# The PSUM banks of attention given out anew, with sample updates and window 0 re-spaced, in a two-layer hybrid decoder step

## The chip, the cores and the metric

One core of a Trainium2 chip runs the whole step in one launch. The metric is the time of one execution on the device in microseconds (us), median of several runs. The kernel is written engine by engine: TensorE (PE; its weight loads are shown apart as PEld), VectorE (DVE), ScalarE (ACT), and SyncE (SP), whose queue starts most transfers. Each engine works off its own instructions strictly in order, and all waiting between engines is by semaphores set by hand. GpSimd has nothing to do in the stretches below.

## The reference, cut to what matters

One inference step over 1024 new prompt tokens and 32 sample tokens (8 sequences of 4), width 1024, all in fp32. Layer 0 is gated linear attention (4 heads) and a convolutional feed-forward layer; layer 1 is sliding-window attention (window 128, 16 heads of 64, 2 key/value heads, a learned bias, one sink per head) and another conv-FFN. Every sub-layer has a norm before and after it. The parts touched:

```python
def step(S, inp):                       # linear attention, per chunk
    ...
    S_new = jnp.exp(b_last)[..., None] * S + jnp.einsum('bchk,bchv->bhkv', k_dec, vi)
...
def sink_attend(q, k, v, bias, valid, sinks):
    s = jnp.einsum('bqngd,bknd->bngqk', q, k).astype(jnp.float32) * ATT_HEAD_DIM ** -0.5 + bias
    s = jnp.where(valid, s, -jnp.inf)
    m = jnp.maximum(jnp.max(s, axis=-1, keepdims=True), sink)
    p = jnp.exp(s - m)
    denom = jnp.sum(p, axis=-1, keepdims=True) + jnp.exp(sink - m)
    return jnp.einsum('bngqk,bknd->bqngd', (p / denom).astype(v.dtype), v)
```

The output of attention goes through an output projection (w_o_b) and is added to the residual stream after a norm.

## The kernel before, in words

**Matrix products.** Every fp32 product is made of three matmuls in the reduced type fp32r: low weights by high activations, high by low, high by high. The weights come as 366 blocks of 128 x 1024. For each, SP loads it (w_load, L407, a ring of two), ACT rounds it to the high half (w_round, L415), DVE subtracts to get the low half (w_rest, L420); high and low have a ring of three blocks. `project` (L431, matmuls L437) multiplies one block by the token stream; `down_unit` (L450, L460) makes one unit of an output (down) projection from two blocks into one PSUM bank, and `down_add` (L464, L470 and L472) has DVE add it to the accumulator. Tokens stand in two halves, X = 0 (512 tokens, one chunk) and X = 1 (512 and the 32 samples, two chunks of 272). PSUM has 8 banks, PS[:, 0] to PS[:, 7].

**Linear attention.** Eight turns u: 4 heads times 2 halves; in turns 4 to 7 (X = 1) each of the 8 sample sequences also updates its state. On PE, `turn` (L698) ends with outputs, then `sample_deltas` (L781, L788) for sequences 0 to 3, half of the next turn's first value projection, sequences 4 to 7, the sum of squares over partitions (L844 to L847, matmuls with ones, L846; it waits for DVE's fold, gq_f) and the second half of the projection. The products alternate between banks 6 and 7, so product b waits for update b-2. DVE makes the eight updates (L1049 to L1053, L1052), then the fold (L1055). ACT goes on with the norm's logarithm and exponential (L1242, L1244). In the last turn the first FFN block stands in the place of the next projection (`pe_first_block`).

**Attention.** 64 steps, g: 16 pairs of heads q (8 for each half of the tokens, since X = 0 and X = 1 are walked one after the other) times 4 blocks of 128 tokens. The loop over steps s (L1751) makes windows of 8 steps, s = 8k + w. On PE step s has scores(s) (L1630, banks 0 and 1), a part of a query projection if w < 4 (query 2k+1 in w = 0, 1; 2k+2 in w = 2, 3; L437, banks 5 and 6), transposed(s-2) of the probabilities (L1642, banks 2 and 3 in turn), a quarter of the output projection of window k-1 if w >= 4 (downs, L1660, banks 6 and 7 in turn, each waiting until the unit two before has been added), and values(s-3) (L1656, bank 4). DVE has lo(s-4) (L1832, low half of the output), divided(s-1) (L1825, the reciprocal), biased(s) (L1818: adds the bias and takes the negated maximum in one reduction; L1811 copies the sink), low halves of weights, and the accumulations. ACT has hi(s-4) (L1998), scaled(s-1) (L1976, probabilities by the reciprocal), exps(s) (L1967, which waits until transposed(s-2) has read the same buffer, tf), turned(s-2) (L1989, transposed probabilities from PSUM to SBUF), query copies (L1955), and the roundings of weights. In the windows from k = 4 the norm of a half is interleaved with this by tables (ACT_AT, DVE_AT, PE_AT, L1580 to L1590): squares and roots, with the table loads of Ln and Exp on ACT (L520, L522).

**Sample softmax.** In windows k = 4 to 7 (d = k - 4) the 32 sample tokens' attention over their caches stands among the steps, all as one tile of 128 x 1056. PE: s_scores (L1710) in w = 4, 5, s_transposed (L1732, L1734) in w = 0 to 2 of the next window, s_values (L1743). DVE: s_new (L1847), s_add (L1853), s_masked (L1859, L1861) in w = 5, 6, s_max (L1865 to L1870) in w = 7, s_scaled (L1874 to L1878) in w = 0 of the next window, after the two low halves of output weights. ACT: s_exps (L2020, L2021) in w = 7, after the roundings of `downs_done`.

**The head of attention.** act_att (L1939) begins with the rounding of a query block, the roundings behind layer 0's last down projections (`act_ffn_downs_done`), the wait for the convolution state's output, and only then query(0). SP (sp_rest, L2128), at the block ("aq", 0, 2), waits for the last down projection of layer 0 (dn_full) before it loads the attention bias (L2088) and constants (L2152), whose buffers lie on the FFN's; the weight blocks behind stand in the same queue.

## Time and profile before

| | us |
|---|---|
| median of 3 runs (lowest, highest) | 2677.86 (2673.72, 2679.54) |
| the profiled execution, its own time | 2676.1 |
| its span in the trace | 2674.3 |
| PE busy | 2510.8 (94% of the span) |
| PEld busy | 2195.8 (82%) |
| DVE busy | 1624.0 (61%) |
| ACT busy | 1145.8 (43%) |
| mean granted clock of TensorE | 0.971 |

The linear attention takes about the first 700 us, the first conv-FFN runs to 1429, attention from there to about 1890, the second conv-FFN to the end. A row "PE banks L1732 <- DVE s_scores L1878: 6.8, 2, 3.8" in the view of waits says that PE, before instructions of line 1732 that write banks, waited 6.8 us in all in 2 places, the longest 3.8, for DVE's line 1878. In a timeline each row has start, duration, engine, line, operation, out<-in and count, and in brackets the idle time before it and who ended it.

### The profile page before, as it was taken

How to read it: one execution, taken by the hardware profiler on the slowest of the kernel's cores; microseconds unless marked ns; L12 is line 12 of the kernel's file. 1: busy time of each engine (PE TensorE's matmuls, PEld its weight loads, DVE VectorE, ACT ScalarE, POOL GpSimd, SP SyncE). 2: the span in 40 equal slices, each digit the busy share in tenths (PEclk: the TensorE clock that was granted, in tenths of full speed). 3: DMA queues.
4: the chain of work that ended last, by engine and by line, in shares of the span. 5: the costliest groups of instructions: out<-in, count | busy, mean ns of one | idle time of the engine just before them, and what ended most of it. 6: DMA issues, size and time to landing. Idle time of an engine off the chain costs nothing. (4 is left out here: it accounts for less than half of the span.)

```text
span 2674.3 us, 37812 instructions
## 1 busy us (share of the span) xinstructions
PE 2510.8 (94%) x15455; PEld 2195.8 (82%) x15455; DVE 1624.0 (61%) x2928; ACT 1145.8 (43%) x1810; POOL 0.2 (0%) x4
## 2 busy tenths in 40 slices
PE   7999999998999999999997899888999999999997
PEld 5778888887778889999996577766788888999996
DVE  5676656575656556766655655564676555655556
ACT  5554453443443334343334656563434333323333
POOL 0000000000000000000000000000000000000000
PEclk9999999899999999999998899999999999999999
DMA  4221222223433323322323222230342322333222
GB/s 153 65 77 64 88 95 84 95 81 109 149 102 109 100 91 101 133 80 95 95 76 102 90 92 64 85 97 26 107 146 93 95 95 95 103 119 95 87 87 95
DMA packets 93434, 255.18 MB, mean 95 GB/s; under 512 B 12500, under 2 KB 43709, under 8 KB 91325
## 3 DMA queue, kind: packets, MB, share of 16 engines
q1 hardware_dynamic: 69980, 209.24, 24.6%
q10 hardware_dynamic: 23280, 43.52, 4.7%
q8 instruction: 123, 2.02, 0.3%
q14 instruction: 51, 0.41, 0.1%
HBM read 225.92 MB, written 26.74 MB: 94 GB/s over the span
## 5 line engine op out<-in xcount | busy, mean ns | idle before, releaser
L437 PE MATMUL banks<-act_hi,w_lo 128*128 128x272 f32 (+1 forms) x2952 | 984.1, 333 | 29.8 <-DVE w_lo L420 13.0
L437 PE MATMUL banks<-act_hi,w_hi 128*128 128x272 f32 (+1 forms) x2952 | 969.1, 328 | 0.0
L437 PE MATMUL banks<-act_lo,w_hi 128*128 128x272 f32 (+1 forms) x2952 | 967.7, 328 | 0.0
L415 ACT ACTIVATE w_hi<-w_raw 128x1024 fp32r<-128x1024 f32 x366 | 380.7, 1055 | 716.5 <-PE banks L460 491.1
L420 DVE TENSOR_TENSOR w_lo<-w_raw,w_hi 128x1024 fp32r<-128x1024 f32 x366 | 442.7, 1223 | 395.9 <-ACT w_hi L415 395.5
L437 PEld LDWEIGHTS banks<-act_hi,w_lo 128*128 128x128 f32 x2952 | 567.0, 192 | 96.2 <-issue 33.5
L437 PEld LDWEIGHTS banks<-act_lo,w_hi 128*128 128x128 f32 x2952 | 567.9, 192 | 44.6 <-issue 1.7
L437 PEld LDWEIGHTS banks<-act_hi,w_hi 128*128 128x128 f32 x2952 | 566.3, 192 | 44.9
L472 DVE TENSOR_TENSOR acc<-acc,banks 128x272 f32<-128x272 f32 (+1 forms) x624 | 315.3, 519 | 194.4 <-PE banks L460 191.2
L460 PE MATMUL banks<-h_hi,w_lo 128*128 128x272 f32 (+1 forms) x1056 | 346.2, 328 | 25.5 <-DVE acc L472 12.6
L460 PE MATMUL banks<-h_hi,w_hi 128*128 128x272 f32 (+1 forms) x1056 | 344.2, 326 | 0.0
L460 PE MATMUL banks<-h_lo,w_hi 128*128 128x272 f32 (+1 forms) x1056 | 343.8, 326 | 0.0
L460 PEld LDWEIGHTS banks<-h_hi,w_lo 128*128 128x128 f32 x1056 | 199.1, 189 | 48.5 <-DVE acc L472 16.5
L460 PEld LDWEIGHTS banks<-h_lo,w_hi 128*128 128x128 f32 x1056 | 200.7, 190 | 16.5
L460 PEld LDWEIGHTS banks<-h_hi,w_hi 128*128 128x128 f32 x1056 | 199.4, 189 | 15.5
L1497 ACT ACTIVATE u<-banks 128x512 f32<-128x512 f32 (+2 forms) x132 | 59.6, 451 | 191.4 <-PE banks L437 188.5
L1511 ACT ACTIVATE c<-u,par 128x512 f32<-128x512 f32 (+1 forms) x88 | 73.1, 831 | 70.7 <-issue 69.1
L1419 DVE SCALAR_TENSOR_TENSOR c<-u,par,c 128x512 f32<-128x512 f32 (+1 forms) x88 | 68.1, 774 | 46.4 <-ACT c L1511 46.4
L1967 ACT ACTIVATE probs<-scores,stats 128x257 f32<-128x257 f32 (+1 forms) x128 | 62.3, 488 | 60.6 <-PE banks L1642 51.6
L460 PE MATMUL banks<-o_hi,w_lo 128*128 128x272 f32 (+1 forms) x192 | 67.6, 352 | 21.4 <-DVE acc L472 12.1
L1387 DVE TENSOR_TENSOR h_lo<-hf,h_hi 128x512 fp32r<-128x512 f32 (+1 forms) x88 | 62.1, 705 | 34.8 <-ACT h_hi L1544 34.8
L1544 ACT ACTIVATE h_hi<-hf 128x512 fp32r<-128x512 f32 (+1 forms) x88 | 56.0, 637 | 59.5 <-DVE hf L1445 30.0
(232 smaller groups left out, 2596.5 us busy)
## 6 DMA issues: line engine op xcount, KB each, us to landing
w_raw<-wall SPq DMA_DIRECT2D x366, 512.0 KB, 3.6
normed<-h_scratch ACTq DMA_DIRECT2D x20, 352.0 KB, 3.8
h_scratch<-acc ACTq DMA_DIRECT2D x3, 2176.0 KB, 7.7
h_scratch<-acc ACTq DMA_DIRECT2D x3, 2048.0 KB, 8.3
gstates<-state ACTq DMA_DIRECT2D x4, 1024.0 KB, 6.3
gla_s<-gstates ACTq DMA_DIRECT2D x4, 1024.0 KB, 4.2
bias<-bias_scratch SPq DMA_DIRECT2D x32, 128.0 KB, 3.4
bias_scratch<-bias_rows SPq DMA_DIRECT2D x8, 383.0 KB
```

The costliest lines, as they stand in the source:

```text
L415: nc.scalar.activation(WH[:, b % RING], WR[:, b % RAW], ACT.Copy).then_inc(w_hi, 1)
L420: nc.vector.tensor_tensor(WL[:, b % RING], WR[:, b % RAW], WH[:, b % RING].bitcast(fp32), ALU.subtract).then_inc(w_lo, 1)
L437: last = nc.tensor.matmul(PS[:, bank, 0:n], w, a[X][:, k, o:o + n], start=(k == 0 and first), stop=(k == KT - 1 and w is wh and a is AH))
L460: last = nc.tensor.matmul(PS[:, bank, 0:w_], w, a[t][:, o:o + w_], start=(t == 0 and x == 0), stop=(t == 1 and x == 2))
L472: nc.vector.tensor_tensor(a, a, PS[:, bank, 0:w_], ALU.add).then_inc(dn_add, 1)
L1387: nc.vector.tensor_tensor(HL[:, t % 2, 0:W], HF[:, t % 2, 0:W], HH[:, t % 2, 0:W].bitcast(fp32), ALU.subtract).then_inc(hl, 1)
L1419: nc.vector.scalar_tensor_tensor(C[:, 0:cv], U[:, 1:1 + cv], PAR[:, t, 17:18], C[:, 0:cv], ALU.mult, ALU.add).then_inc(cv1, 1)
L1497: last = nc.scalar.activation(U[:, 2 + o:2 + end], PS[:, bank, 0:end - o], ACT.Copy)
L1511: nc.scalar.activation(C[:, 0:cv], U[:, 2:2 + cv], ACT.Identity, bias=PAR[:, t, 19:20], scale=PAR[:, t, 18:19]).then_inc(cb, 1)
L1544: nc.scalar.activation(HH[:, t % 2, 0:WX[X]], HF[:, t % 2, 0:WX[X]], ACT.Copy).then_inc(hh, 1)
L1967: last = nc.scalar.activation(EX[:, u, e, x0:], SS[:, u, e, x0:], ACT.Exp, bias=ST[:, r, 2 + e:3 + e], scale=-1.0, accum_out=ST[:, r, 4 + ...
```

## The change

The buffers of attention are laid out in another order (probabilities with three buffers in place of two), so that q1, bias and the others fall on other FFN buffers. The transposed probabilities have bank 2 alone: transposed(g) waits for turned(g-1). exps(g) waits for transposed(g-3). The output projections take turns on banks 3, 6 and 7 and wait for the unit three before. In the sample turns of linear attention the updates go two at a time between quarters of the projection, the sum of squares follows the second quarter, and on DVE the fold stands between the fourth and the fifth update. At the head, query(0) on ACT comes before the roundings behind the last down projections, and SP waits for the hidden state of the last half's tiles (hl) instead of the last down projection. In window 0 queries 1 and 2 are spread over steps 0 to 6. In the sample softmax the sinks are negated once, mask and negated maximum are two reductions in place of six operations, the exponential moves from w = 7 to w = 6 and the scaling from w = 0 of the next window to w = 7. On DVE divided(s-1) comes before lo(s-4).

```diff
@@ -256,11 +256,12 @@
+        PT = place("probs_t", [P, 2, 4, P])
+        EX = place("probs", [P, 3, 2, NBW])
+        SS = place("scores", [P, 2, 2, NBW])
+        BI = place("bias", [P, 2, 2, 2 * WIN])
         Q1 = place("q1", [P, 2, WM])
-        BI = place("bias", [P, 2, 2, 2 * WIN])
-        SS = place("scores", [P, 2, 2, NBW])
-        EX = place("probs", [P, 2, 2, NBW])
-        PT = place("probs_t", [P, 2, 4, P])
         FFN_END = arena + 2 * WM * 4 * 2 + 2 * HUW * 4 * 2 + 2 * WM * 4 + (20 + 18 + 2) * FT * 4 + 8 * 32
@@ -829,28 +830,28 @@
                 outputs(3)
-                if X:
-                    sample_deltas(0, 4)
+                for y in range(4):
+                    ks = range(2 * y, 2 * y + 2)
+                    if X:
+                        sample_deltas(2 * y, 2 * y + 2)
+                    if y == 0:
+                        if more:
+                            pe.wait_ge(s_upd, 4 * u + 4)
+                        if X:
+                            pe.wait_ge(os_ev, h + 1)
+                    if more:
+                        value(u + 1, 0, ks)
+                    else:
+                        pe_first_block(pe, 0, "u", ks)
+                    if y == 1:
+                        pe.wait_ge(gq_f, u + 1)
+                        for c, (o, w_) in enumerate(CHUNKS[X]):
+                            last = nc.tensor.matmul(PS[:, 2 + c, 0:w_], ones[:], SQ0[:, 0, o:o + w_], start=True, stop=True)
+                        last.then_inc(gq_ss, 1)
                 if more:
-                    pe.wait_ge(s_upd, 4 * u + 4)
-                    if X:
-                        pe.wait_ge(os_ev, h + 1)
-                    value(u + 1, 0, FIRST)
-                else:
-                    pe.wait_ge(os_ev, h + 1)
-                    pe_first_block(pe, 0, "u", FIRST)
-                if X:
-                    sample_deltas(4, NB)
-                pe.wait_ge(gq_f, u + 1)
-                for c, (o, w_) in enumerate(CHUNKS[X]):
-                    last = nc.tensor.matmul(PS[:, 2 + c, 0:w_], ones[:], SQ0[:, 0, o:o + w_], start=True, stop=True)
-                last.then_inc(gq_ss, 1)
-                if more:
-                    value(u + 1, 0, SECOND)
                     pe.wait_ge(gq_ms, u + 1)
...
                 else:
-                    pe_first_block(pe, 0, "u", SECOND)
                     pe.wait_ge(gq_ms, u + 1)
@@ -1047,14 +1055,13 @@
                 if X:
-                    for b in range(NB):
-                        dve.wait_ge(ss_full, 8 * h + b + 1)
-                        nc.vector.scalar_tensor_tensor(SB[:, b], SB[:, b], EL[:, 8 + b:9 + b], PS[:, 6 + b % 2, 0:DV],
-                                                       ALU.mult, ALU.add).then_inc(ss_upd, 1)
+                    samples(0, 4)
                 dve.wait_ge(gq_sq, u + 1)
...
                     dve_step(dve, *step)
+                if X:
+                    samples(4, NB)
                 if more:
@@ -1575,6 +1582,10 @@
+        def down_bank(k, m):
...
+            return (3, 6, 7)[(DN[group(k)] + m) % 3]
@@ -1589,6 +1600,10 @@
+        FIRST_QUERIES = {0: (1, range(0, 3)), 1: (1, range(3, 6)), 2: (1, range(6, 8))} | {3 + y: (2, range(2 * y, 2 * y + 2)) for y in range(4)}
+        QUERY_DONE = {1: 2, 2: 6} | {q: 8 * ((q - 1) // 2) + (1 if q % 2 else 3) for q in range(3, PAIRS)}
@@ -1634,12 +1649,12 @@
                 pe.wait_ge(sc, g + 1)
-                if g >= 2:
-                    pe.wait_ge(te, g - 1)
+                if g:
+                    pe.wait_ge(te, g)
                 for e in range(2):
...
                         m = 2 * e + k
-                        last = nc.tensor.transpose(PS[:, 2 + g % 2, m * P:(m + 1) * P], EX[:, g % 2, e, k * WIN:(k + 1) * WIN],
+                        last = nc.tensor.transpose(PS[:, 2, m * P:(m + 1) * P], EX[:, g % 3, e, k * WIN:(k + 1) * WIN],
                                                    ident[:])
@@ -1674,7 +1689,7 @@
                               [OH1[:, (2 * k + t) % 3] for t in range(2)], [OL1[:, (2 * k + t) % 3] for t in range(2)],
-                              6 + m % 2, 2)
+                              down_bank(k, m), 3)
@@ -1755,7 +1770,10 @@
                     pe.wait_ge(dn_add, dn_end((1, FG - 1)))
-                if w < 2 and k < 8:
+                if k == 0:
+                    if w in FIRST_QUERIES:
+                        query(*FIRST_QUERIES[w])
+                elif w < 2 and k < 8:
                     query(2 * k + 1, (FIRST, SECOND)[w])
@@ -1800,6 +1818,8 @@
             dve.wait_ge(sn, 1)
+            nc.vector.tensor_scalar(SKS[:], SKS[:], -1.0, None, ALU.mult).then_inc(sn, 1)
+            dve.wait_ge(sn, 2)
@@ -1837,7 +1857,7 @@
                 for m in units:
-                    down_add(dve, X, group(k), m, 6 + m % 2, k % 4 == 0)
+                    down_add(dve, X, group(k), m, down_bank(k, m), k % 4 == 0)
@@ -1855,19 +1875,14 @@
                 dve.wait_ge(xsa, 3 * d + 3)
-                nc.vector.tensor_tensor(SX[:, 0:SEQ].rearrange("p (b k) -> p b k", b=NB),
-                                        SX[:, 0:SEQ].rearrange("p (b k) -> p b k", b=NB), bc(BM4[:], WIN), ALU.add)
-                nc.vector.tensor_tensor(SX[:, SEQ:T], SX[:, SEQ:T], SM4[:], ALU.add).then_inc(xsb, 1)
-
-            def s_max(d):
-                dve.wait_ge(xsb, d + 1)
-                nc.vector.tensor_reduce(SST[:, 0:1], SX[:], AX.X, ALU.max).then_inc(xmx, 1)
-                dve.wait_ge(xmx, 3 * d + 1)
-                nc.vector.tensor_tensor(SST[:, 0:1], SST[:, 0:1], SKS[:, d:d + 1], ALU.max).then_inc(xmx, 1)
-                dve.wait_ge(xmx, 3 * d + 2)
-                nc.vector.tensor_tensor(SST[:, 2:3], SKS[:, d:d + 1], SST[:, 0:1], ALU.subtract)
-                nc.vector.tensor_scalar(SST[:, 1:2], SST[:, 0:1], -1.0, None, ALU.mult).then_inc(xmx, 1)
+                nc.vector.tensor_tensor_reduce(SX[:, 0:SEQ].rearrange("p (b k) -> p b k", b=NB),
+                                               SX[:, 0:SEQ].rearrange("p (b k) -> p b k", b=NB), bc(BM4[:], WIN), -1.0,
+                                               SKS[:, d:d + 1], ALU.add, ALU.min, SST[:, 0:1]).then_inc(xsb, 1)
+                dve.wait_ge(xsb, 2 * d + 1)
+                nc.vector.tensor_tensor_reduce(SX[:, SEQ:T], SX[:, SEQ:T], SM4[:], -1.0, SST[:, 0:1], ALU.add, ALU.min,
+                                               SST[:, 1:2]).then_inc(xsb, 1)
@@ -1888,20 +1903,17 @@
                 d = k - 4
+                if 1 <= s <= NIT:
+                    divided(s - 1)
                 if s >= 4 and s % 2 == 1:
                     lo(s - 4)
-                if 1 <= s <= NIT:
-                    divided(s - 1)
                 if s < NIT:
                     biased(s)
-                if w == 2 and k < 8:
-                    rest_after(dve, ("aq", (2 * k + 1) // 8, (2 * k + 1) % 8))
-                    if k == 2:
-                        rest_after(dve, ("kv", 1, 0))
-                elif w == 4 and k < 7:
-                    rest_after(dve, ("aq", (2 * k + 2) // 8, (2 * k + 2) % 8))
-                    if k == 2:
-                        rest_after(dve, ("kv", 1, 1))
+                for q in range(1, PAIRS):
+                    if QUERY_DONE[q] + 1 == s:
+                        rest_after(dve, ("aq", q // 8, q % 8))
+                if k == 2 and w in (2, 4):
+                    rest_after(dve, ("kv", 1, w // 2 - 1))
                 elif w == 0 and k >= 2:
@@ -1909,9 +1921,7 @@
                 if d >= 0:
-                    if w == 0 and d:
-                        s_scaled(d - 1)
-                    elif w == 3 and d:
+                    if w == 3 and d:
                         s_lo(d - 1)
@@ -1919,8 +1929,8 @@
                         s_masked(d)
-                    elif w == 7:
-                        s_max(d)
+                    elif w == 7 and d < 4:
+                        s_scaled(d)
                 if s in DVE_AT:
@@ -1937,11 +1947,6 @@
         def act_att(act):
-            act.wait_ge(q_full, AQ[0, 0, 0])
-            round_after(act, ("aq", 0, 0))
-            act_ffn_downs_done(act, 1, FG - 1)
-            act.wait_ge(cn_out, 16)
-
             def query(q):
@@ -1953,18 +1958,17 @@
                     nc.scalar.activation(Q1[:, q % 2, o:o + w_], PS[:, 5 + c if q else 0, 0:w_], ACT.Copy, scale=HD ** -0.5).then_inc(q_ev, 1)
-                if q:
-                    round_after(act, ("aq", X, p))
+                round_after(act, ("aq", X, p))
...
                 act.wait_ge(sk, 2 * q + min(i, 1) + 1)
-                if g >= 2:
-                    act.wait_ge(tf, g - 1)
+                if g >= 3:
+                    act.wait_ge(tf, g - 2)
                 for e in range(2):
-                    last = nc.scalar.activation(EX[:, u, e, x0:], SS[:, u, e, x0:], ACT.Exp, bias=ST[:, r, 2 + e:3 + e],
+                    last = nc.scalar.activation(EX[:, g % 3, e, x0:], SS[:, u, e, x0:], ACT.Exp, bias=ST[:, r, 2 + e:3 + e],
                                                 scale=-1.0, accum_out=ST[:, r, 4 + e:5 + e])
@@ -2016,9 +2020,9 @@
             def s_exps(d):
-                act.wait_ge(xmx, 3 * d + 3)
-                nc.scalar.activation(SX[:], SX[:], ACT.Exp, bias=SST[:, 1:2], accum_out=SST[:, 4:5])
-                nc.scalar.activation(SST[:, 5:6], SST[:, 2:3], ACT.Exp).then_inc(xex, 1)
+                act.wait_ge(xsb, 2 * d + 2)
+                nc.scalar.activation(SX[:], SX[:], ACT.Exp, bias=SST[:, 1:2], scale=-1.0, accum_out=SST[:, 4:5])
+                nc.scalar.activation(SST[:, 5:6], SKS[:, d:d + 1], ACT.Exp, bias=SST[:, 1:2], scale=-1.0).then_inc(xex, 1)
@@ -2041,7 +2045,10 @@
+            act.wait_ge(hl, FT * 2)
             query(0)
+            act_ffn_downs_done(act, 1, FG - 1)
+            act.wait_ge(cn_out, 16)
             for s in range(NIT + 4):
@@ -2053,18 +2060,17 @@
                     turned(s - 2)
-                if w == 1 and k < 8:
-                    query(2 * k + 1)
-                elif w == 3 and k < 7:
-                    query(2 * k + 2)
-                elif w == 7 and k:
+                for q in range(1, PAIRS):
+                    if QUERY_DONE[q] == s:
+                        query(q)
+                if w == 7 and k:
                     downs_done(k - 1)
...
                 if d >= 0:
-                    if w == 7:
+                    if w == 6:
                         s_exps(d)
@@ -2144,7 +2150,7 @@
                     sp.dma_start(conv_new[0], CN[:]).then_inc(cn_out, 16)
-                    sp.wait_ge(dn_full, dn_end((1, FG - 1)))
+                    sp.wait_ge(hl, FT * 2)
                     sp.wait_ge(rb_out, 16 * 8)
```

## Rows read from the trace of the kernel before

**Rows 1.** Stretches: window length, busy us (PE, PEld, DVE, ACT, POOL), clock, DMA.

```profile
850.00:1420.00 570.00, 563.39 (x3834) 527.69 (x3833) 347.23 (x611) 205.63 (x284) 0.00 (x0) 1.00 0.31 99
...
1440.00:1500.00 60.00, 48.45 (x248) 33.39 (x247) 35.95 (x96) 43.79 (x102) 0.00 (x0) 0.86 0.34 118
...
1500.00:1860.00 360.00, 311.64 (x2131) 242.73 (x2131) 202.82 (x529) 208.75 (x510) 0.00 (x0) 0.93 0.23 72
```

**Rows 2.** L788's idle; PE timeline, turn 5; a stretch, turn 6.

```profile
  DVE gstates L1052: 4.4, 8
...
444.32 1.19 PE L846 MATMUL banks<-gsq,ones 128*128 128x272 f32 x4 [1.21 <-DVE gsq L1055]
...
518.00:531.00 13.00, 11.50 (x46) 8.96 (x47) 5.42 (x10) 5.58 (x6) 0.00 (x0) 0.76 0.03 5
```

**Rows 3.** Timelines of PE, ACT and SP at the head of attention.

```profile
1438.00 0.80 PE L1630 MATMUL banks<-kg,q 64*128 64x128 f32 x4 [8.78 <-issue]
...
1436.36 1.06 ACT L415 ACTIVATE w_hi<-w_raw 128x1024 fp32r<-128x1024 f32 x1 [6.04 <-DMA w_raw<-wall]
...
1438.83 1.28 ACT L1967 ACT_TABLE_LOAD   x1 [0.93 <-DVE scores L1811]
...
1432.47 6.56 SPq L410 DMA_DIRECT2D w_raw<-wall  x3
```

**Rows 4.** View of waits, ACT, 1430 to 1880 (us in total, times, longest).

```profile
ACT probs L1967 <- PE banks L1642: 51.6, 21, 4.8
```

**Rows 5.** View of waits, PE, 1420 to 1880.

```profile
PE banks L460 <- DVE acc L472: 12.1, 7, 3.3
...
PE banks L1732 <- DVE s_scores L1878: 6.8, 2, 3.8
...
PE banks L437 <- ACT q L1955: 5.5, 6, 1.5
...
PE banks L460 <- DVE w_lo L420: 3.1, 1, 3.1
```

**Rows 6.** Timeline of PE, step 5.

```profile
1464.28 1.11 PE L1642 MATMUL banks<-ident,probs 128*128 128x128 f32 x4 [4.92 <-ACT probs L1976]
```

**Rows 7.** Timeline of DVE, step 40: two low halves.

```profile
1671.02 2.36 DVE L420 TENSOR_TENSOR w_lo<-w_raw,w_hi 128x1024 fp32r<-128x1024 f32 x2
```

**Rows 8.** Timelines of DVE, ACT and PE, steps 47 and 48.

```profile
1717.86 0.44 DVE L470 COPY acc<-banks 128x272 f32<-128x272 f32 x1 [0.77 <-PE banks L460]
...
1718.61 0.44 DVE L470 COPY acc<-banks 128x272 f32<-128x272 f32 x1 [0.31 <-PE banks L460]
...
1720.70 1.18 ACT L2020 ACTIVATE s_scores<-s_scores,s_stats 128x1056 f32<-128x1056 f32 x1
...
1724.20 0.56 PE L437 MATMUL banks<-act_hi,w_lo 128*128 128x272 f32 x1 [3.35 <-DVE w_lo L420]
```

**Rows 9.** Lines L1818, L1859: ns lowest/median/highest, first and last start.

```profile
L1818 DVE CUSTOM_DVE_ANT_0 scores<-banks,bias,sinks_b x128: 343/480/486, 1439.0 to 1835.7; 128x256 f32<-128x256 f32 x112, 128x128 f32<-128x128 f32 x16
...
L1859 DVE TENSOR_TENSOR s_scores<-s_scores,s_mask x4: 1224/1226/1226, 1662.7 to 1832.6; 128x1024 f32<-128x1024 f32 x4
```

**Rows 10.** Timelines of PE and ACT: steps 38, 39, 4 and 59.

```profile
1657.29 0.70 PE L1630 MATMUL banks<-kg,q 64*128 64x256 f32 x4
...
1662.50 0.66 PE L1642 MATMUL banks<-ident,probs 128*128 128x128 f32 x4
...
1659.97 0.58 ACT L1989 ACTIVATE probs_t<-banks 128x512 f32<-128x512 f32 x1
...
1457.22 0.66 PE L1642 MATMUL banks<-ident,probs 128*128 128x128 f32 x4
...
1457.44 0.57 ACT L1989 ACTIVATE probs_t<-banks 128x512 f32<-128x512 f32 x1
...
1804.52 0.97 PE L1642 MATMUL banks<-ident,probs 128*128 128x128 f32 x4 [1.60 <-ACT probs L1976]
...
1805.33 0.60 ACT L1989 ACTIVATE probs_t<-banks 128x512 f32<-128x512 f32 x1
```

21 lines of the change are left out of this document (13 added, 8 removed).

## The prediction

> **What bounds the kernel now.** The table of stretches comes first [rows 1]. In the first layer's conv-FFN TensorE is busy 563.39 of 570 us at clock 1.00, so nothing is to be had there. In attention it is busy 48.45 of 60 us at the head, at a clock of 0.86, and 311.64 of 360 us after it, at 0.93. So the bound is TensorE's own order of work, with waits in the linear-attention turns that carry samples, at the head of attention, and in some of the 64 attention steps. Next come TensorE's waits by what released them [rows 5], ACT's [rows 4], and the timelines around the longest ones. A wait of ACT or DVE counts below only as far as a wait of TensorE hangs on it.
>
> The profiled execution took 2676.1 us, 1.8 less than the median of the runs (2677.86); the sum is made against 2676.1. About 0.2%, 5.4 us, is what a measurement can tell from no change.
>
> **A. Sample states.** In turns 4 to 7 eight updates go four at a time on two banks, so the third of four waits for DVE: 4.4 us of TensorE idle in 8 waits. Then the sum of squares waits 1.21 us for DVE's fold, which stands behind all eight updates; each of the four turns has this gap [rows 2]. Two at a time with a quarter of a projection between covers the first wait, the fold ahead of the last four updates the second: 4.4 + 4 × 1.21 = 9.2. I take off 0.25 a turn for the added switches between the two kinds of matmul: 8.2, bounds 5 and 9.2. DVE's last four updates now come behind the fold; the next turn's projection needs their banks only a quarter later, so nothing new is late. The clock is 0.76 over the 13 us around turn 6 [rows 2], a loss of 13 × 0.24 = 3.1, and turn 7 looks the same: 6.2. Some of it should return with shorter waits: 4, bounds 0 and 6.2. **A is 12.2.**
>
> **B. The head.** TensorE's last down projection ends 8.78 us before scores(0) at 1438.00, so at 1429.2 [rows 3]. SP held its queue until then, so the second weight of the last round was issued behind the bias, at 1432.47; ACT waits 6.04 us for it, and copies query(0) only afterwards. The change lets SP go when the second half's hidden state is made, and puts query(0) ahead of ACT's two roundings, so scores(0) can start at about 1429.3. That is not all won: step 0's exponential begins to load its table at 1438.83, and ACT, busy 43.79 of the next 60 us, sets the pace of window 0 [rows 1, 3]. DVE still makes two low halves (2.36 us for two, [rows 7]) ahead of biased(0), so the exponential moves to about 1433.4: 5.4. Spreading queries 1 and 2 over seven steps adds a part of the 4.92 us for which TensorE waits behind query 2's copy, rounding and two table loads [rows 6]: half of it. 5.4 + 2.5 = **8**, bounds 5 (table only) and 12 (most of 8.78 and 4.92).
>
> **C. One bank, three probability buffers.** exps(g) waited for transposed(g-2), now for transposed(g-3): ACT lost 51.6 us in 21 such waits [rows 4]. Most is hidden. TensorE's waits that hang on ACT's lateness are 5.5 for query copies and 3.1 for a low half [rows 5]; ACT is behind by about one of its operations there, so 60% of 8.6 goes: **5**, bounds 2 and 8. The price is the new wait of transposed(g) for turned(g-1). In the step shown scores(38) start at 1657.29, turned(36) ends at 1659.97 + 0.58 = 1660.55 and transposed(37) starts at 1662.50: 1.95 to spare [rows 10]. The same difference is negative in 12 of 63 steps, the first -0.79 (1457.22 against 1457.44 + 0.57), the last -1.41, summing to 9.1 [rows 10]; most are steps in which ACT was late by the waits that go. I take **-1**, bounds 0 and -9.
>
> **D. Third bank for output projections.** TensorE waits 12.1 us in 7 for DVE's accumulation [rows 5]. A third bank lets it go one more unit ahead, 0.75 us (accumulations follow TensorE at 1717.86 and 1718.61, [rows 8]): 7 × 0.75 = 5.3. **5**, bounds 0 (DVE is as late one unit on) and 6.5.
>
> **E and F. Sample softmax.** The transposes of its probabilities wait 6.8 us in two for the scaling [rows 5], which stands behind two low halves (2.36) of the next window [rows 7]. It now comes a step earlier: **6.8**, bounds 4 and 6.8. In step 48 query 13 waits 3.35 us, and the sample exponential (1.18) stands on ACT ahead of the root that the query needs [rows 8]; a step up it frees 1.2 here and at step 56: **2.4**, bounds 1 and 2.4. On DVE the max and its small operations go, and mask and minimum become one reduction. Its nearest row is the biased one, 0.48 us at 256 wide and 0.343 at 128 [rows 9], 1.07 ns an element, so 1.3 at 1024, against 1.226 for the mask alone [rows 9]: no dearer than before, on work that TensorE doesn't wait for.
>
> **The cost of moving.** The exponential at w=6 holds ACT until DVE has masked, so scaled, exps and turned of the next step come up to 1.5 later, four times; DVE's scaling at w=7 delays its accumulations there. The 1.95 to spare covers most [rows 10]: **-4**, bounds -2 and -9. DVE's divided ahead of lo is in this.
>
> **G. Clock.** From 1440 to 1860 the loss is 60 × 0.14 + 360 × 0.07 = 34 us [rows 1]. About half follows waits that the change shortens, though few of them go entirely. **6**, bounds 0 and 15.
>
> The sum is 12.2 + 8 + 5 - 1 + 5 + 6.8 + 2.4 - 4 + 6 = 40.4. D, E and F lie in the same windows, where a wait that goes uncovers the next one (a low half or an accumulation late by the time won): 2.4 off. **Forecast: 2676.1 - 38 = 2638 us.**
>
> **Rivals.**
> *The waits only move on (0.22).* ACT and DVE set the windows' length, so B, C, D and F return nothing and the clock doesn't recover: 8.2 + 6.8 = 15, 2661 us. For it: ACT's 43.79 of 60 [rows 1]. Against: later it is busy 208.75 of 360, and most of its waits are for TensorE's transposes [rows 1, 4]. The Trainium skill's "TensorE: Matmul & The Clock Gate" (HAM oscillation — how this bites in real kernels) has a kernel to which PSUM double-buffering gave no further gain; that would be this rival's case for D, and against it stand the 12.1 us waited for banks here [rows 5].
>
> *The clock stays up (0.12).* The waits alone give 40.4 - 4 - 6 = 30.4; with 6.2 and 15 of the clock it is 51.6 and 2624.5 us, with the upper bounds of B and C 2617.5. For it: the low stretches lie where the waits are. Against: waits of over 1 us remain.
>
> *The transposes become a chain (0.07, slower).* With one bank, turned(g-1) must end before transposed(g), and ACT does it only after exps(g+1). It decides from the point where ACT is more than 1.95 us behind its place in most steps: at 0.7 us a step, 64 × 0.7 = 45, and 2638 + 45 = 2683 us. For it: 12 steps of 63 would be late at the old times. Against: from scores to turned the chain is 3.3 us (1657.29 to 1660.55, [rows 10]), where a step takes 6.6 on average (420 us / 64), and exps is let go earlier.
>
> *No effect that can be told (0.06).* The new waits cost their outer bounds (-9 and -9) and B, C, D, F and the clock return 3 to 5 in all: 15 + 4 - 18, so 2675 us.
>
> **How the numbers follow.** The forecast has 0.53, with 2618 to 2656 as its own range. Faster by over 0.2% is 0.53 + 0.22 + 0.12 = 0.87; within it 0.06; slower 0.07. The range, 2608 to 2664, takes in the first two rivals and leaves out the other two and the tails.
>
> **What would show it.** Right: no 1.2 us gap ahead of the sum of squares in turns 4 to 7; scores(0) within 1 us of the last down projection; exps waiting for transposed under 15 us; no transpose of sample probabilities waiting over 1 us; waits for accumulations near 6 us. Wrong: transposed waiting for turned by over 10 us in all, new waits for low parts behind w=7, or a window 0 that ends no more than 4 us earlier.

## The result, and the profile after

The changed kernel takes 2630.31 us, the median of 4 runs (2627.02 to 2634.45), against 2678.14 before (4 runs): a ratio of 0.9825 with a 95% interval of 0.9806 to 0.9844, 47.8 us less. The profiled execution took 2628.7 us, with a span of 2626.9 and a mean clock of 0.981. In the code after, lines up to the sample updates are one higher, and attention's lie some 15 to 30 lower in the file (scores L1645, transposed L1657, values L1671, biased L1838, lo L1852, exps L1971, turned L1990 and L1993).

The span is cut where the work can be matched: from the first sample update to the last down projection of layer 0 (sample turns and conv-FFN), and from scores(0) to the end of values(63). The table of stretches for the kernel before (length; busy us of PE, PEld, DVE, ACT, POOL; clock; DMA):

```profile
352.51:1429.22 1076.71, 1039.86 (x6484) 940.82 (x6483) 667.10 (x1113) 415.92 (x557) 0.00 (x0) 0.97 0.31 100
1438.00:1854.73 416.73, 356.83 (x2340) 273.38 (x2340) 239.73 (x629) 253.17 (x609) 0.00 (x0) 0.92 0.25 79
```

and for the kernel after:

```profile
352.56:1412.72 1060.16, 1029.70 (x6484) 931.92 (x6483) 666.45 (x1113) 416.72 (x558) 0.00 (x0) 0.98 0.32 103
1412.72:1806.34 393.62, 347.59 (x2341) 265.57 (x2340) 236.71 (x624) 255.82 (x611) 0.00 (x0) 0.95 0.27 85
```

The first stretch is 16.6 us shorter (1076.71 to 1060.16). Between the two lay 8.78 us [rows 3]; now nothing does. Attention is 23.1 shorter (416.73 to 393.62): TensorE's idle time there, length less busy, fell from 59.9 to 46.0, and its busy time by 9.2 with the same matmuls, which is the clock (0.92 to 0.95). 16.6 + 8.8 + 23.1 = 48.5, and what lies before and behind is 1.1 longer. So some 19 us of the 48 are a higher clock (10.2 of PE's busy time in the first stretch, 9.2 in attention), and 29 are waits (6.4, 8.8 and 13.9). The clock is no accident of the one profile: its mean is 0.979 to 0.982 in the four runs of the changed kernel, and 0.967 to 0.975 in the 41 runs of the kernel before that stood beside the experiments (one slow execution, 4065.85 us at 0.556, is left out).

The head, timelines of PE, ACT and PE again:

```profile
1412.72 0.49 PE L1645 MATMUL banks<-kg,q 64*128 64x128 f32 x4
...
1412.83 2.01 ACT L416 ACTIVATE w_hi<-w_raw 128x1024 fp32r<-128x1024 f32 x2 [11.00 <-PE banks L461]
1417.22 1.28 ACT L1971 ACT_TABLE_LOAD   x1 [2.38 <-DVE stats L1838]
...
1417.21 0.70 PE L1645 MATMUL banks<-kg,q 64*128 64x256 f32 x4 [1.52 <-DVE stats L1838]
```

scores(0) follows without a gap, both roundings go in one piece (2.01, no wait for a DMA), and the table load of the first exponential starts 4.5 us behind the last down projection, where before it was 9.6 (1438.83 less 1429.2, [rows 3]). The new 1.52 us at scores(1) is the wait for biased(0), behind two low halves on DVE.

TensorE's waits in attention (us, times, longest):

```profile
PE banks L1671 <- DVE o_lo L1852: 9.0, 7, 2.5
PE banks L461 <- DVE acc L473: 8.1, 6, 2.8
PE banks L438 <- ACT q L1960: 6.5, 4, 3.1
PE banks L1645 <- DVE stats L1838: 5.4, 7, 1.5
PE banks L1657 <- ACT probs_t L1993: 4.7, 3, 3.1
...
PE banks L461 <- DVE acc L471: 2.1, 1, 2.1
...
PE banks L1657 <- ACT probs_t L1990: 0.8, 1, 0.8
```

two of ACT's waits:

```profile
ACT probs_t L1993 <- PE banks L1657: 28.1, 17, 5.4
...
ACT s_scores L2024 <- DVE s_stats L1884: 13.5, 4, 3.8
```

and of the kernel before, two that stand against the first and the fourth of these, and one that has no row any more:

```profile
PE banks L1656 <- DVE o_lo L1832: 9.1, 5, 2.8
...
PE banks L1630 <- DVE stats L1818: 1.5, 5, 0.6
...
PE banks L1642 <- ACT probs L1976: 6.5, 2, 4.9
```

Against [rows 5]: the 6.8 us of sample transposes waiting for the scaling are gone, the accumulations went from 12.1 to 8.1 (from 13.2 to 10.2 with the first groups of the halves). The 6.5 us in which transposed waited for scaled, 4.92 of them in [rows 6], are gone too. Scores now wait 5.4 us for biased, where it was 1.5, and transposed 5.5 for turned (4.7 + 0.8), where it was none; the waits for low parts are what they were, 9.0 against 9.1, but at other steps. The 51.6 us of exps waiting for transposed [rows 4] are gone; ACT now waits 28.1 us in turned and 13.5 for the sample masking.

At step 39 the wait for the low part is long. Timelines of DVE, ACT and PE:

```profile
1633.07 1.29 DVE L1880 CUSTOM_DVE_ANT_1 s_scores<-s_scores,s_mask,s_sinks 128x1024 f32<-128x1024 f32 x1
...
1634.70 1.18 ACT L2024 ACTIVATE s_scores<-s_scores,s_stats 128x1056 f32<-128x1056 f32 x1 [3.82 <-DVE s_stats L1884]
...
1636.06 1.89 ACT L494 ACTIVATE normed<-acc 128x2048 f32<-128x2048 f32 x1
...
1638.25 0.42 DVE L1852 TENSOR_TENSOR o_lo<-banks,o_hi 128x256 fp32r<-128x256 f32 x1 [3.51 <-ACT o_hi L2002]
...
1638.82 0.67 PE L1671 MATMUL banks<-probs_t,v_tok 128*64 128x128 f32 x8 [2.52 <-DVE o_lo L1852]
```

The fused reduction takes 1.29 us. ACT stands 3.82 us before the sample exponential, then does the norm's square (1.89), only then the high half, and DVE's low half waits 3.51 for it, TensorE 2.52 for that.

In the sample turns TensorE's matmuls wait neither for the fold nor for a bank any more. The views of lines L849 (sum of squares) and L789 (updates) still have 0.5 us of idle time in 3 places, for the fold, and 3.2 in 12 that end for nothing the profile shows; both are of the weight loads (PEld), which have rows of their own beside the matmuls. Taken for PE alone, neither line has any.

### The profile page after: what moved, and what is told of

Read it like the earlier page. It is cut to its first block and busy times, and to the rows that moved or that the text cites. A ratio compares the mean times of both kernels' runs of the same rounds, so it can differ in the third digit from the quotient of the medians.

```text
span 2626.9 us, 37815 instructions
## 1 busy us (share of the span) xinstructions
PE 2492.7 (95%) x15455; PEld 2180.2 (83%) x15455; DVE 1618.0 (62%) x2921; ACT 1146.9 (44%) x1810; POOL 0.2 (0%) x4
## 5 line engine op out<-in xcount | busy, mean ns | idle before, releaser
L438 PEld LDWEIGHTS banks<-act_hi,w_lo 128*128 128x128 f32 x2952 | 561.0, 190 | 95.2 <-issue 38.1
L438 PEld LDWEIGHTS banks<-act_lo,w_hi 128*128 128x128 f32 x2952 | 562.1, 190 | 43.4 <-issue 1.7
L461 PEld LDWEIGHTS banks<-h_lo,w_hi 128*128 128x128 f32 x1056 | 201.8, 191 | 16.6
L1838 DVE CUSTOM_DVE_ANT_0 scores<-banks,bias,sinks_b 128x256 f32<-128x256 f32 (+1 forms) x128 | 54.4, 463 | 43.1 <-issue 20.0
L461 PE MATMUL banks<-o_hi,w_lo 128*128 128x272 f32 (+1 forms) x192 | 66.8, 348 | 13.9 <-DVE acc L473 7.8
```

Source lines behind the costliest of these rows:

```text
L438: last = nc.tensor.matmul(PS[:, bank, 0:n], w, a[X][:, k, o:o + n], start=(k == 0 and first), stop=(k == KT - 1 and w is wh and a is AH))
L461: last = nc.tensor.matmul(PS[:, bank, 0:w_], w, a[t][:, o:o + w_], start=(t == 0 and x == 0), stop=(t == 1 and x == 2))
L1838: last = nc.vector.tensor_tensor_reduce(SS[:, u, e, x0:2 * WIN], PS[:, e, x0:2 * WIN], BI[:, q % 2, e, x0:], -1.0, SINK[:, 2 * (q % 8) + e ...
```

## The experiments

Twelve kernels were run. For each its two stretches are shown as above, when they bear on it; "attention" is the second of them, and "idle" is length less PE's busy time. Ratios are against the kernel before, run beside each. The times of one kernel's runs lie 7 us apart (2627.02 to 2634.45 above) and up to 14 (2668.98 to 2682.96, 17 runs of the kernel before), so small effects are read from the stretches, each of one profile.

**Linear attention alone** (`gla_only`): the kernel before with the change's edits of `turn` and of DVE's samples:

```diff
-                    sample_deltas(0, 4)
...
+                for y in range(4):
+                    ks = range(2 * y, 2 * y + 2)
+                    if X:
+                        sample_deltas(2 * y, 2 * y + 2)
...
+                    samples(0, 4)
                 dve.wait_ge(gq_sq, u + 1)
...
+                    samples(4, NB)
```

> Only part A: the kernel before, with the sample updates two at a time, the fold ahead of the last four and the sum of squares behind the second quarter. Theory (the parts are local and add up): the stretch from the first sample update to the end of linear attention is 16 to 18 us shorter, as in the changed kernel, attention stays as it was, and the time is about 2661. Rival (part of the gain in this stretch comes from elsewhere, or the clock only rose by chance in the one profile): 6 to 9 us shorter, the waits alone, about 2670.

Measured: 2664.7 us (ratio 0.9955, 0.9941 to 0.9968).

```profile
354.00:1416.86 1062.86, 1031.03 (x6484) 933.96 (x6483) 666.51 (x1113) 416.30 (x557) 0.00 (x0) 0.98 0.32 102
1425.68:1842.20 416.52, 357.72 (x2340) 273.69 (x2340) 239.75 (x629) 253.27 (x609) 0.00 (x0) 0.92 0.26 79
```

The first stretch is 13.9 us shorter, less than the theory's 16 and more than the rival's 9; attention is as before (416.52). So the part is local. Its idle time falls by 5.0 (36.9 to 31.8), the busy time by 8.8. The 2.7 us that are missing against the changed kernel's 16.6 can be chance: such stretches differ by up to 7 us (last section).

**The sum of squares alone** (`gla_sum_only`):

```diff
+                pe.wait_ge(gq_f, u + 1)
+                ...
+                last.then_inc(gq_ss, 1)
                 if X:
                     sample_deltas(4, NB)
-                pe.wait_ge(gq_f, u + 1)
-                ...
```

with DVE's updates split around the fold.

> Half of part A: the updates stay four at a time, only the fold and the sum of squares go ahead of the last four. Of the waits this takes 4.8 us (four gaps of 1.21) and leaves the 4.4 us of updates that wait for their bank. If the clock falls because of the 1.2 us gaps: about as good as the whole of A, 13 to 16 us. If it falls because of the updates themselves (a row of narrow matmuls with waits between): 5 to 7 us, and the granted clock of the turns stays at 0.91 to 0.94.

Measured: 2663.83 us (0.9952, 0.9936 to 0.9968).

```profile
352.53:1415.62 1063.09, 1030.20 (x6484) 933.21 (x6483) 666.87 (x1113) 416.19 (x557) 0.00 (x0) 0.98 0.32 102
```

13.6 us shorter: nearly the whole of the part. Two updates at a time add 0.2 us to it, 1.1 of idle time (32.9 to 31.8). The reason lies in how [rows 2] was read: the 4.4 us in 8 waits are idle time of the weight loads (PEld). Taken for PE alone L788 has no wait for DVE, in the kernel before or here, and 1.1 us of small gaps in all. Eight matmuls of updates take 2.40 us, and four in 1.13 when they go two at a time (turn 6, the kernel before and `gla_only`):

```profile
517.91 2.40 PE L788 MATMUL banks<-gv,gkd_masked 32*128 32x256 f32 x8
...
514.23 1.13 PE L788 MATMUL banks<-gv,gkd_masked 32*128 32x256 f32 x4
```

The 20 us from the first update of turn 6, in the kernel before and in this run:

```profile
517.91:537.91 20.00, 18.50 (x100) 15.95 (x100) 9.77 (x16) 10.22 (x10) 0.00 (x0) 0.83 0.22 86
...
512.83:532.83 20.00, 19.71 (x134) 17.41 (x134) 12.24 (x19) 12.07 (x12) 0.00 (x0) 1.00 0.33 113
```

In such 20 us of turns 4 to 7 the clock was 0.83, 1.00, 0.83 and 0.74, and is 1.00, 1.00, 1.00 and 0.99 here, where the updates still go four at a time. So in three of the four turns it fell with the 1.2 us gap or with what follows it, and not with the rows of updates.

**The head alone** (`head_only`): buffers, SP's wait, and on ACT

```diff
-            act.wait_ge(q_full, AQ[0, 0, 0])
-            round_after(act, ("aq", 0, 0))
-            act_ffn_downs_done(act, 1, FG - 1)
-            act.wait_ge(cn_out, 16)
...
+            act.wait_ge(hl, FT * 2)
             query(0)
+            act_ffn_downs_done(act, 1, FG - 1)
+            act.wait_ge(cn_out, 16)
```

> Only the head of part B: buffers laid out anew, SP let go by the hidden state, query(0) ahead of the roundings; queries 1 and 2 not spread, nothing else. Theory: scores(0) starts within 1 us of the last down projection (8.6 us won) and 5 to 9 of it are left at the first score of window 1, since ACT is the pace of window 0: about 2670. Rival (window 0 gives it all back): scores(0) earlier by 8.6, window 1 earlier by no more than 2.

Measured: 2669.41 us (0.9974, 0.9961 to 0.9986), 8.2 us less than the 2677.62 of before beside it. Stretches of windows 0 and 1:

```profile
1429.67:1467.22 37.55, 26.01 (x137) 17.08 (x137) 25.80 (x66) 28.82 (x63) 0.00 (x0) 0.90 0.38 121
1467.22:1519.61 52.39, 42.74 (x217) 30.42 (x217) 29.84 (x74) 33.56 (x74) 0.00 (x0) 0.88 0.21 75
```

Against before (scores(0) at 1438.00, window 1 from 1475.1) scores(0) starts 8.3 us earlier and window 1 7.9: window 0 gives back 0.5. Attention as a whole is 417.86 us here, 1.1 longer than before, with 3.1 more of idle time.

**Three buffers of probabilities** (`after_ex2`): EX[:, g % 3] back to g % 2, and

```diff
-                if g >= 3:
-                    act.wait_ge(tf, g - 2)
+                if g >= 2:
+                    act.wait_ge(tf, g - 1)
```

> The changed kernel with two buffers of probabilities: exps(g) waits for transposed(g-2) again; banks as in the changed kernel. Theory: ACT's waits of exps for transposed come back at 40 to 50 us, TensorE's waits for query copies, roots and low halves grow by 3 to 6 us, mostly in windows 0 to 4, and the time by as much. Rival (these waits are hidden whichever buffer there is): under 2 us.

Measured: 2641.58 us (0.9866, 0.9845 to 0.9886).

```profile
1412.77:1817.88 405.11, 350.41 (x2341) 267.41 (x2340) 237.51 (x624) 253.50 (x611) 0.00 (x0) 0.95 0.26 83
...
ACT probs L1971 <- PE banks L1657: 51.7, 22, 6.2
```

ACT's wait is back to the tenth, and attention is 11.5 us longer (405.11 against 393.62), 8.7 of it idle. So these waits were not hidden, and the theory's 3 to 6 was half of it. TensorE's waits show where they come out (in the changed kernel 4.7 in 3, and 6.5 in 4):

```profile
PE banks L1657 <- ACT probs_t L1993: 8.9, 8, 3.1
PE banks L438 <- ACT q L1960: 8.5, 7, 3.1
```

Scores wait 1.1 more for biased and roots 1.0 more. The largest of these, 4.2 us, is the wait for turned(g-1), which the one bank of the transposes brings; what a third buffer is worth with two banks for them was not run.

**The third bank** (`after_downs67`):

```diff
-            return (3, 6, 7)[(DN[group(k)] + m) % 3]
+            return 6 + m % 2
...
-                              down_bank(k, m), 3)
+                              down_bank(k, m), 2)
```

> The changed kernel with the output projections back on two banks (6 and 7, waiting for the unit two before); the transposed probabilities keep their one bank. Theory: without the third bank TensorE's waits for the accumulations, 8.1 + 2.1 us in the changed kernel, grow by 0.75 us each, 4 to 6 us in all, and the time by as much. Rival (the waits only move on: DVE's lateness decides, not the number of banks): they change by less than 2 us and the time not at all.

Measured: 2642.37 us (0.9868, 0.9852 to 0.9883).

```profile
1417.39:1821.47 404.08, 349.49 (x2341) 269.01 (x2340) 237.61 (x624) 256.62 (x611) 0.00 (x0) 0.95 0.27 83
...
PE banks L461 <- DVE acc L473: 14.7, 8, 3.6
...
PE banks L461 <- DVE acc L471: 3.3, 2, 2.8
```

Attention is 10.5 us longer, 8.6 of it idle; the waits for accumulations are 18.0 in place of 10.2 (within attention 16.4 in place of 9.4), and those for roots 2.7 more. The third bank is worth twice what was forecast, in a kernel that keeps one bank for the transposes.

**Both bank changes undone** (`after_old_banks`): as the last, and

```diff
-                if g:
-                    pe.wait_ge(te, g)
+                if g >= 2:
+                    pe.wait_ge(te, g - 1)
...
-                        last = nc.tensor.transpose(PS[:, 2, m * P:(m + 1) * P], ...
+                        last = nc.tensor.transpose(PS[:, 2 + g % 2, m * P:(m + 1) * P], ...
```

> The changed kernel with both bank changes undone: two banks for the transposed probabilities (transposed(g) waits for turned(g-2)) and two for the output projections. Against the run with the projections alone undone it shows the price of the one bank. Theory: the waits of transposed for turned (4.7 + 0.8 us in the changed kernel) go nearly all, 3 to 5 us of TensorE's idle, but most of it comes back one instruction later as a wait of values for the low part or of turned itself, so this is 1 to 3 us faster than the projections alone undone. Rival (the chain of transposes is what holds attention now): 6 us or more faster.

Measured: 2637.62 us (0.9850, 0.9834 to 0.9866).

```profile
1411.85:1810.24 398.39, 345.99 (x2341) 266.14 (x2340) 237.31 (x624) 256.25 (x611) 0.00 (x0) 0.95 0.27 84
```

Against the run before it attention is 5.7 us shorter, 2.2 of it idle and 3.5 clock. The clock's part can't be told from chance, nor can 1.6 of the idle time: a place of 1.9 us that ends for nothing the profile shows is 0.3 here (last section). By TensorE's waits the theory holds: the 5.6 us of transposes waiting for turned are gone, and 3.0 more for low parts and 1.5 for the scaling stand in their place. So the one bank costs about 1 us by its waits and not over 6 by the times, the third bank brings 10.5, and giving the banks out anew is worth 4.8 us of attention together (398.39 to 393.62), 6.4 of idle time.

**The sample softmax's order** (`after_softmax_back`): 

```diff
-                    if w == 6:
+                    if w == 7:
                         s_exps(d)
...
+                    if w == 0 and d:
+                        s_scaled(d - 1)
...
-                    elif w == 7 and d < 4:
-                        s_scaled(d)
```

> The changed kernel with the sample softmax's exponential back in w=7 (behind the roundings) and its scaling back in w=0 of the next window; the fused reductions stay. Theory: transposes of sample probabilities wait for the scaling again, 6 to 7 us in steps 40 and 59, query 13's and 15's blocks wait 2 to 3 more at steps 48 and 56, while the 2.5 us stall at step 39 goes: 5 to 9 us slower, from step 39 on. Rival (moving it only shifts the wait): within 2 us.

Measured: 2635.16 us (0.9842, 0.9822 to 0.9862).

```profile
1415.13:1810.90 395.77, 348.38 (x2341) 267.89 (x2340) 236.60 (x624) 256.00 (x611) 0.00 (x0) 0.94 0.27 85
...
PE banks L1747 <- DVE s_scores L1893: 4.4, 2, 2.9
```

The wait for the scaling is back with 4.4 us, and query blocks at steps 48 and 56 wait 5.2 more (3.3 in place of 0.4 for a root, 2.3 in place of none for a low half). But low parts wait 3.3 less, accumulations 2.5 and query copies 0.9, and attention is only 2.2 longer, 1.4 of it idle (3.0 without the place of 1.9 us named above, which is 0.3 here too). The whole time is 4.9 longer, with intervals that overlap. That is less than the theory's 5 to 9 and about the rival's size: most of what was won at steps 40, 48, 56 and 59 was spent at step 39 and its like.

**Where it was spent** (`after_exps_late`, then `after_exps_behind_hi`): the exponential first behind the norm's square in w=6, then at the start of w=7:

```diff
                         act_step(act, *pass_at(s), name, SUM_BANK.get(s))
+                if d >= 0 and w == 6:
+                    s_exps(d)
```

```diff
                     hi(s - 4)
+                if d >= 0 and w == 7 and d < 4:
+                    s_exps(d)
...
-                    if w == 6:
-                        s_exps(d)
-                    elif w < 3 and d:
+                    if w < 3 and d:
```

> The changed kernel with one order altered: in w=6 the sample exponential stands behind the norm's square on ACT instead of ahead of it (this matters in step 38 alone). Theory: in the changed kernel ACT waits 3.82 us for the masking at step 38 and makes the square only afterwards, so the output's high half, its low half and values(36) are late by 2.52 us; with the square first this stall shrinks by 1.5 to 1.9, and the time by 1 to 2 us. Rival (the wait is DVE's, not ACT's): the stall stays within 0.3.

> The changed kernel with the sample exponential on ACT at the start of w=7, behind hi(s-4) and ahead of scaled(s-1), instead of at the end of w=6. In the changed kernel hi stands behind it, DVE's lo behind hi, and the accumulations behind lo, so TensorE waits at steps 39 (2.52), 47 (2.06), 55 (2.84) and 63 (2.05). Theory (that chain is the cost of moving): steps 39, 47 and 63 lose 1.2 to 2 us of their wait each, step 55 little, since DVE is busy with the norm there; 3 to 5 us of TensorE's idle in all, and the time 3 to 5 us below the changed kernel. Rival (DVE is late by its own work at w=7): less than 1.5 us.

Measured: 2628.73 (0.9820, 0.9793 to 0.9846) and 2629.06 us (0.9818, 0.9804 to 0.9832). The wait of values(36) at step 39 in the first of them, and its attention:

```profile
PE banks L1671 <- DVE o_lo L1852: 0.7, 1, 0.7
...
1416.15:1808.00 391.85, 345.53 (x2341) 264.35 (x2340) 236.63 (x624) 255.78 (x611) 0.00 (x0) 0.96 0.27 86
```

and of the second its attention, the wait for the accumulations of the second half's first group, and PE's wait at step 48:

```profile
1417.87:1807.62 389.75, 346.88 (x2341) 265.56 (x2340) 236.38 (x624) 255.65 (x611) 0.00 (x0) 0.95 0.27 86
...
PE banks L461 <- DVE acc L471: 0.2, 1, 0.2
...
1690.99 0.57 PE L438 MATMUL banks<-act_hi,w_lo 128*128 128x272 f32 x1 [2.87 <-ACT rstd L521]
```

In the first 2.52 became 0.7, as the theory had it. The 1.8 us by which attention is shorter is not this, though: idle time is 46.3 against 46.0, and the difference is busy time, the clock. Accumulations wait 1.5 us more and roots 2.0 more, so here waits came up elsewhere for what was won. The second takes 3.9 us off attention against the changed kernel, 3.2 of it idle and 1.6 of that by chance (the place of 1.9 us). Steps 39 and 47 (2.06 down to 0.2) are free, step 63 is 0.7 better and step 55 the same; at step 48 a wait of 2.87 for the root takes part of it back, and a new one of 1.38 for an accumulation. As whole times, neither can be told from the changed kernel, so no better version is claimed.

**Window 0** (`after_late_q2`, `after_queries_back`): the first has the exponential behind the square, as above, makes query 2 in bank 3 and drops its wait for query 1's copy,

```diff
-                        if c == 0 or q != 8:
+                        if q != 2 and (c == 0 or q != 8):
                             pe.wait_ge(q_ev, ...
...
-                    project(pe, X, BLK["aq", X, p], c, 5 + c if q else 0, q_full, ks)
+                    project(pe, X, BLK["aq", X, p], c, 3 if q == 2 else 5 + c if q else 0, q_full, ks)
```

the second takes the spread out:

```diff
-                if k == 0:
-                    if w in FIRST_QUERIES:
-                        query(*FIRST_QUERIES[w])
-                elif w < 2 and k < 8:
+                if w < 2 and k < 8:
```

> The changed kernel with the sample exponential behind the norm's square (as in the run before) and with query 2 made in bank 3, which window 0 doesn't use, so that it needn't wait until ACT has copied query 1 out of bank 5. In the changed kernel TensorE waits 3.10 us there, at step 3 of window 0. If ACT is the pace of window 0, as the prediction has it, the 3 us of TensorE are idle one or two steps later and window 0 stays at 36.1 us within 0.7. If the wait for the bank decides, window 0 is 2 to 3 us shorter. Whole time against the run before: 0 to 3 us.

> The changed kernel without the spreading of window 0: queries 1 and 2 in halves in steps 0 to 3, as before. Theory: the spread covers part of ACT's lateness at step 5; without it window 0 (36.1 us) is 1 to 2.5 longer, as in the run with the head alone (37.6), and nothing else changes. Rival (the spread does nothing, or costs by the later roundings): within 0.5.

Measured: 2628.22 (0.9812, 0.9793 to 0.9831) and 2632.26 us (0.9831, 0.9811 to 0.9851). Windows 0 and 1 of the changed kernel,

```profile
1412.72:1448.81 36.09, 25.96 (x138) 17.08 (x137) 24.82 (x66) 28.82 (x63) 0.00 (x0) 0.91 0.34 106
1448.81:1502.38 53.57, 43.85 (x217) 31.33 (x217) 31.23 (x75) 33.66 (x73) 0.00 (x0) 0.87 0.24 87
```

window 0 of the first,

```profile
1416.68:1453.16 36.48, 26.98 (x137) 17.20 (x137) 24.74 (x66) 28.93 (x63) 0.00 (x0) 0.91 0.33 105
```

and windows 0 and 1 of the second:

```profile
1420.68:1458.42 37.74, 27.02 (x138) 17.59 (x137) 25.98 (x67) 28.92 (x63) 0.00 (x0) 0.85 0.39 119
1458.42:1507.35 48.93, 41.45 (x216) 29.55 (x217) 29.87 (x74) 33.45 (x73) 0.00 (x0) 0.91 0.22 81
```

With the 3.10 us wait gone window 0 is 36.48 against 36.09: transposes now wait 4.6 us for turned in it, where it was 0.8. With two banks for the transposes (`after_old_banks`) it is 36.76. So neither bank holds window 0. That is what a window paced by ACT, on which both waits hang, would show. Without the spread window 0 is 1.65 longer, as expected, but window 1 is 48.93 against 53.57 (and 50.09 in the first), so that the two together are not longer, nor is their idle time (18.2 against 19.9). Over all of attention it is 392.84 us without the spread, with 42.9 of idle time against 46.0. The spread gives nothing that can be shown.

**DVE's order** (`after_lo_first`): lo(s - 4) again ahead of divided(s - 1).

```diff
+                if s >= 4 and s % 2 == 1:
+                    lo(s - 4)
                 if 1 <= s <= NIT:
                     divided(s - 1)
-                if s >= 4 and s % 2 == 1:
-                    lo(s - 4)
```

> The changed kernel with DVE's lo(s-4) ahead of divided(s-1) again. In it ACT's scaled waits for divided, divided stands behind lo, and lo for ACT's hi. Theory: a small cost, 0 to 3 us, in steps with odd s, where ACT's scaled comes 0.4 us later; the waits of values for the low part (9.0 us) get smaller by 1 to 3 us at the same time. Rival (the order is a condition for the one bank, since transposed hangs on scaled): 4 us or more slower.

Measured: 2633.2 us (0.9829, 0.9808 to 0.9850).

```profile
1418.26:1812.79 394.53, 347.67 (x2341) 266.39 (x2340) 236.16 (x624) 256.84 (x611) 0.00 (x0) 0.95 0.27 85
```

0.9 us in attention (394.53 against 393.62): in the theory's bounds, and too little to be told from nothing.

## Why the prediction was right, and where its terms were off

The forecast was 38 us, the measured gain 47.8, inside the range. Its waits came to 28 us and its clock to 10; measured are 29 and 19. So the time lies about as near to the rival "The clock stays up" (30.4 and 21) as to the forecast. That the waits add up so well is in part luck: C and D were worth double, and the waits of A and the moves of the sample softmax about half. By its own steps:

- **A, 12.2.** Measured alone 13.9, by two errors of opposite sign: the waits gave 5.0 of idle time in place of 8.2, and the clock 8.8 in place of 4. The step that failed is the 4.4 us of [rows 2], read as idle time of TensorE's matmuls; it is that of the weight loads, and "Two at a time with a quarter of a projection between covers the first wait" gives 1.1. No run shows the 0.25 a turn taken off for switches between matmuls: in `gla_only` PE is busy for all of the 20 us from the first update of each turn. Nearly all comes from the fold and the sum going first, 4.0 us of it idle time (36.9 to 32.9) and 9.7 clock. The clock was low in turn 4 as well, which the sum left out.
- **B, 8.** Scores(0) came 8.3 us earlier with the head alone, 7.9 of it kept at the start of window 1. The prediction kept only what the first exponential moves, 5.4; its table load moved by 4.9 (1438.83 to 1433.91), and window 0 yet lasted only 0.5 longer. So a late start of ACT is mostly made good within the window, and the first exponential doesn't set what is kept. The half of 4.92 us that the spread was to add is not there, and the two errors nearly cancel.
- **C, 5 and -1.** The third buffer is worth 11.5 as measured by its loss, 8.7 of it idle. The step that failed is the choice of waits: 60% of 8.6 us for query copies and one low half. Query copies wait 6.5 in the changed kernel, where it was 5.5, and the low half 2.0 in place of 3.1. The largest part of the gain is elsewhere: without the buffer transposes wait 9.3 for turned in place of 5.5. The price of the one bank, 1, agrees with its waits, and the times allow up to 6.
- **D, 5.** Measured 10.5. The step that failed is "one more unit ahead, 0.75 us": without the bank there are 10 waits in place of 7, 7.8 us more in all, and 1.9 of clock go with them. Its sign, waits for accumulations near 6 us, did not come true either: 10.2 are left, some of them brought by the moved exponential at w=7 (2.06 us at step 47). The kernel in the Trainium skill's "TensorE: Matmul & The Clock Gate" (HAM oscillation — how this bites in real kernels) to which PSUM double-buffering gave no further gain doesn't describe this place: here a third bank gave 10.5.
- **E and F less the cost of moving, 5.2.** Measured 2.2, 1.4 to 3.0 of it idle. The gains were as forecast, 4.4 and 5.2 for 6.8 and 2.4; the cost was 6.7 in place of 4. The exponential at the end of w=6 stands ahead of the square and of hi, as the two runs with it elsewhere show at steps 39 and 47. The forecast had named scaled, exps and turned as late, not hi, which is the one that counted; the "new waits for low parts behind w=7", its own sign of being wrong, are there. The reduction took 1.29 us, as worked out from the biased rows. If the rule in the Trainium skill's "Vector Engine (DVE) Microarchitecture Reference" (7. Points that are easy to get wrong), which the page states for `S2S2D2_STT`, held for this instruction, it would have been about 2.6 (an estimate, twice the 1.3). The trace does not show that: two fp32 sources in SBUF with an accumulator ran at 1.26 ns an element. Whether the instruction is of that form, no run shows.
- **G, 6.** Busy time in attention fell by 9.2.

The parts tested in attention are worth 4.8 (banks), 11.5 (buffers), 2.2 (softmax), 0.9 (order) and -0.8 (spread, 392.84 to 393.62), 18.6 of 23.1, and the early head costs 1.1. These numbers hold the chance of the clock. By idle time, less the places that end for nothing the profile shows, they are 7.8, 8.7, 2.8, 0.8 and -1.7, together 18.4. Attention lost 15.5 and the early head cost 3.1, together 18.6. So the tested parts account for the waits, as far as taking a part out of the changed kernel measures it. The fused reductions were in every run that had the rest and were not taken apart; little is left for them.

Of the rivals, "the waits only move on" holds for most of E and F, for the spread and for window 0, and not for C and D. "The clock stays up" came nearly true: 19 us of clock in all, where the forecast had 10 and that rival 21. "The transposes become a chain" did not happen: transposed waits 5.5 us in 4 of 63 steps.

## What to carry to other kernels

A wait of an engine off the critical path is hidden only as long as nothing that it delays is: ACT's 51.6 us in exps looked nearly harmless by the waits of TensorE that named a query copy or a low half, and 51.7 like them were worth 11.5 in the changed kernel. When an instruction moves in an in-order queue, go through what then stands behind it at each step, not only what waits for it: the sample exponential shortened the waits at steps 48 and 56 and lengthened those at 39, 47 and 63. Before counting a row of idle time, look whether it is of the matmuls or of the weight loads: 4.4 us of the latter were worth 1.1. And where a bank is short, it may pay to take it from a queue that is turned over once a step and give it to one whose consumer falls behind, as here (the accumulations); one kernel shows this.

## What the runs showed of the hardware

The same instructions didn't get the same clock. Eleven profiled kernels with the whole of part A have first stretches of 1059.11 to 1066.56 us, with PE busy 1026.70 to 1036.00, and window 1 is 53.57 us at clock 0.87 in the changed kernel and 50.38 at 0.93 in `after_exps_late`, which differs only from step 38 on:

```profile
1452.24:1502.62 50.38, 40.67 (x216) 28.92 (x217) 30.95 (x75) 33.55 (x73) 0.00 (x0) 0.93 0.25 92
```

So a gain of 3 us by the clock in one profile shows nothing; idle time agreed far better, 9.72 us in that window against 9.71. It has its chance too: of the ten profiles with the changed attention, four (the changed kernel, `after_downs67`, `after_ex2`, `after_lo_first`) have a place of 1.9 us, at 1507.74 in the changed kernel, that ends for nothing the profile shows. In the other six it is 0.3, among them three whose instructions are the same up to there; the cause stays open.
